# A last combine by column halves, and a gate unit whose products run as three passes

## The reference

```python
def expert_choice_ffn(h, w_router, w_gate, w_up, w_down):
    aff = softmax(h @ w_router)                          # 512 x 16
    gates, idx = top_k(aff.T, 64)                        # 64 tokens for each expert
    xe = h[idx]
    ye = (silu(xe @ w_gate[e]) * (xe @ w_up[e])) @ w_down[e]
    return zeros_like(h).at[idx].add(ye * gates)

x = x + expert_choice_ffn(rms_norm(x, norm_ffn), w_router, w_gate, w_up, w_down)
g = sigmoid(rms_norm(x, norm_ple) @ w_ple_gate)          # 1024 x 1024: the "gate unit"
e = rms_norm(p @ w_ple_proj, norm_ple_post)
x = x + g * e
```

## Time and profile before

| what | us |
|---|---|
| median of 3 executions | 2024.95 |
| lowest and highest of them | 2019.79, 2026.97 |
| span of the profiled execution, first to last instruction | 2020.3 |
| PE busy | 1916.6 |
| DVE busy | 842.5 |
| ACT busy | 577.4 |

### The profile page before, as it was taken

How to read it: one execution, slowest core, us unless ns; L and a number is a source line. 1 busy time by engine, 2 the same in 40 slices (tenths; PEclk the granted TensorE clock), 3 DMA queues, 4 the chain that set the end, 5 groups by cost and what they waited for, 6 DMA issues and landing times.

```text
span 2020.3 us, 22646 instructions
## 1 busy us (share of the span) xinstructions
PE 1916.6 (95%) x9101; PEld 1138.6 (56%) x9101; DVE 842.5 (42%) x1264; ACT 577.4 (29%) x912; POOL 37.4 (2%) x40
## 2 busy tenths in 40 slices
PE   8999899999999989899998999999999999999999
PEld 6667533332233233223323377888888788778887
DVE  6885511111111101111111166466566675886544
ACT  5563400000000000000000055443133434357761
POOL 1022000000000000000000000000000000000000
PEclk9999899999999999999999999999999999999999
DMA  8533699999999999999999954545245222221101
GB/s 268 167 100 138 250 403 429 428 429 428 429 429 428 429 428 430 428 429 429 428 429 428 422 177 159 184 153 190 87 166 172 80 85 82 84 74 53 43 22 42
DMA packets 105109, 528.13 MB, mean 261 GB/s; under 512 B 6998, under 2 KB 52884, under 8 KB 80340
## 3 DMA queue, kind: packets, MB, share of 16 engines
q1 hardware_dynamic: 102420, 520.55, 64.4%
q0 software_dynamic: 1008, 3.52, 0.7%
q10 hardware_dynamic: 1616, 3.15, 0.4%
HBM read 524.97 MB, written 2.23 MB: 261 GB/s over the span
## 4 chain that ended last, share of the span: by engine, by line
PE 68%; DMA 21%; DVE 6%; ACT 3%; issue 1%; ACTq 0%; DVEq 0%
DMA w_expert<-in_w_up 21%; PE bank L1206 11%; PE bank L1195 8%; PE bank L941 5%; PE bank L943 5%; PE bank L942 5%; PE bank L918 5%; PE bank L920 5%; PE bank L919 5%; PE bank L1168 3%; DVE full L1954 2%; PE bank L960 1%; DVE w_lo L1874 1%; PE bank L1418 1%; PE bank L1216 1%
## 5 line engine op out<-in xcount | busy, mean ns | idle before, releaser
L1195 PE MATMUL bank<-w_expert,chosen 128*64 128x512 f32 x2048 | 468.3, 598 | 59.5 <-DMA w_expert<-in_w_up 44.0
L1195 PEld LDWEIGHTS bank<-w_expert,chosen 128*64 128x64 f32 x2048 | 136.8, 136 | 372.0 <-issue 271.3
L2154 DVE TENSOR_TENSOR x_res<-x_res,bank 128x512 f32<-128x512 f32 x136 | 87.1, 683 | 422.4 <-PE bank L1216 402.3
L1206 PE MATMUL bank<-w_expert,hidden_t 128*64 128x512 f32 x1024 | 226.8, 595 | 4.6 <-ACT hidden_t L1662 4.6
L1874 DVE TENSOR_TENSOR w_lo<-raw,w_hi 128x2048 fp32r<-128x2048 f32 x74 | 170.2, 2301 | 113.0 <-ACT w_hi L1465 113.0
L1465 ACT CAST w_hi<-raw 128x2048 fp32r<-128x2048 f32 x74 | 141.0, 1905 | 129.3 <-PE bank L943 123.4
L2176 DVE TENSOR_TENSOR hidden_rows<-gate_silu,bank 128x512 f32<-128x512 f32 x32 | 20.5, 684 | 350.4 <-PE bank L1195 350.4
L918 PE MATMUL bank<-act_hi,w_hi 128*128 128x512 f32 x408 | 166.2, 407 | 0.1
L920 PE MATMUL bank<-act_hi,w_lo 128*128 128x512 f32 x408 | 159.1, 390 | 0.0
L919 PE MATMUL bank<-act_lo,w_hi 128*128 128x512 f32 x408 | 159.0, 390 | 0.0
L1206 PEld LDWEIGHTS bank<-w_expert,hidden_t 128*64 128x64 f32 x1024 | 75.6, 137 | 132.5 <-issue 123.6
(11 more groups left out here) (321 smaller groups left out, 2494.1 us busy)
## 6 DMA issues: line engine op xcount, KB each, us to landing
w_expert<-in_w_gate SPq DMA_DIRECT2D x64, 2048.0 KB, 35.3
w_expert<-in_w_up SPq DMA_DIRECT2D x64, 2048.0 KB, 32.4
w_expert<-in_w_down SPq DMA_DIRECT2D x64, 2048.0 KB, 34.1
raw<-in_a_w_in SPq DMA_DIRECT2D x24, 1024.0 KB, 6.6
raw<-in_b_w_in SPq DMA_DIRECT2D x16, 1024.0 KB, 5.3
raw<-in_a_ada_w SPq DMA_DIRECT2D x12, 1024.0 KB, 5.3
raw<-in_b_ada_w SPq DMA_DIRECT2D x12, 1024.0 KB, 6.0
raw<-in_kv_ada_w SPq DMA_DIRECT2D x8, 1024.0 KB, 5.4
```

The lines of the kernel that those rows point to most:

```text
L1195: last = mm(PS[b0 + n][HALF[x], :], XE[:, k % 4, HALF[k // 4]], WE[place][:, c0:c0 + 512], start=(k == 0), stop=(k == KD - 1), skip_group_ ...
L1206: last = mm(PS[4][HALF[x], :], HT[:, 4 * q + k, HALF[half]], WE[place][:, c0:c0 + 512], start=(i == 0 and k == 0), stop=(i == 7 and k == 3 ...
L2154: tt(part, part, ps[:, :], ALU.add).then_inc(d_add, 1)
```

## The change

Four things are changed. (1) The last expert's combine runs its eight matmuls by half first and then by tile, so that bank j holds half j // 4 and tile j % 4. (2) DVE's eight adds follow that order (`by_half=True`); inside the loop nothing changes. (3) norm(2) waits for as many adds as its column half needs: four before chunks 0 to 3 and eight before chunks 4 to 7, whatever the tile. (4) The first gate unit is no longer `tm_unit` but `first_gates`: for each slab three passes, high by high, high by low, low by high. Within a pass the chunks kc are outside and the four tiles inside. The first pass waits for `hi_ready` and `f_hi`, the second for `lo_ready`, the third for `f_lo`. `begin` is called for each tile at the very first chunk. Banks, slabs, semaphores and the count of 96 matmuls are as before.

```diff
@@ norm(k)
                         if k == 2:
-                            pe.wait_ge(d_add, ADDS - 8 + max(chunks[-1] + 1, 2 * t + 2))
+                            pe.wait_ge(d_add, ADDS - 8 + chunks[-1] + 1)
@@ behind the expert loop, PE
-            for t in range(NT):
-                for x in range(2):
-                    mm(PS[2 * t + x][:, :], SELT[HALF[x], t * P:(t + 1) * P], Y[HALF[x], :], start=True, stop=True
+            for x in range(2):
+                for t in range(NT):
+                    mm(PS[NT * x + t][:, :], SELT[HALF[x], t * P:(t + 1) * P], Y[HALF[x], :], start=True, stop=True
                        ).then_inc(m_c, 1)
             norm(2)
-            for h in range(2):
-                tm_unit(W_PGATE[h], [("pgate", h, t) for t in range(NT)], AH, AL, from_lo(18) if h == 0 else None)
+            def first_gates():
+
+                banks = []
+                for s in range(2):
+                    w = W_PGATE[0][s]
+                    hi, lo = w_hi(w), w_lo(w)
+                    pe.wait_ge(hi_ready, w + 1)
+                    for n, (x, weights) in enumerate(((AH, hi), (AH, lo), (AL, hi))):
+                        if n == 1:
+                            pe.wait_ge(lo_ready, w + 1)
+                        for kc in range(4 * s, 4 * s + 4):
+                            if n != 1:
+                                pe.wait_ge(f_lo if n else f_hi, 18 + kc + 1)
+                            for t in range(NT):
+                                key = ("pgate", 0, t)
+                                if s == 0 and n == 0 and kc == 0:
+                                    banks.append(begin(key, ends_next=False))
+                                last = mm(banks[t][:, :], x[:, kc, t * P:(t + 1) * P], weights[:, kc % 4 * 512:(kc % 4 + 1) * 512],
+                                          start=(s == 0 and n == 0 and kc == 0), stop=(n == 2 and kc == KD - 1))
+                                if n == 2 and kc == KD - 1:
+                                    ends(key)
+                                    last.then_inc(filled, 1)
+                    if s == 0:
+                        last.then_inc(half_used, 1)
+
+            first_gates()
+            tm_unit(W_PGATE[1], [("pgate", 1, t) for t in range(NT)], AH, AL)
@@ DVE
-            def add_combined(j, base_, ps):
+            def add_combined(j, base_, ps, by_half=False):
 
-                t, h = j // 2, j % 2
+                t, h = (j % NT, j // NT) if by_half else (j // 2, j % 2)
                 dve.wait_ge(m_c, base_ + (j + 1))
@@ DVE, behind the expert loop
             for j in range(8):
-                add_combined(j, 8 * NE, PS[j])
+                add_combined(j, 8 * NE, PS[j], by_half=True)
             split_upto(W_PGATE[0][0])
```

## The result

The changed kernel has a median of 2026.57 us over 14 executions (2022.5 to 2029.43), the kernel before 2022.9 over 14 (2019.79 to 2026.97). The ratio is 1.0015 with a 95% interval of 1.0008 to 1.0022: 3.0 us slower, between 1.6 and 4.5 (the two medians lie 3.7 apart). That is within 0.3%, as forecast, and on the slow side.

What follows compares the result with a forecast made beforehand. The prediction took PE, waiting at the seam for DVE's queue, to bound the kernel. Combine 0.96 plus banks 1.33 gave +2.3 us on a median of 2024.95, so 2027.2, range 2021.1 to 2031.9.

Steps and rivals of the forecast that it cites:

- The bound: At the seam PE waits for DVE's gapless queue of adds, slab and remainders, which sets when the first gate unit starts.
- Part 1: Last combine: the new order breaks PE's side-by-side pairs, so DVE's last add starts 0.96 us later.
- the two overlap cases: Last combine: last add 0.79 us later with full overlap of the halves, 0.96 if PE starts matmuls in order.
- the middle case: Last combine: matmuls start in order, only the halves' neighbours overlap; combine 6.0 us, last add 0.96 later.
- the signs given: Timeline marks expected afterwards, among them a combine of about 6.2 us with drain and eight adds of about 5.8.
- rival (b): Seam: first pass starts on ACT's chunks and the combine is not stretched; 1.1 us faster, 2023.8; chance 0.04.
- Part 2: Adds and norm(2): earlier waits gain nothing; transposes begin when PE's combine ends and take 3.6 us.
- Part 3: First gate pass: matmuls 1 to 4 each wait for a remainder to free their bank, 0.669 us apart; 1.33 lost.
- rival (c): Gate unit: granted clock falls to its lower level between 1169 and 1197; 2029.0, or 2049 if lasting; chance 0.06.
- Part 4: Behind the first unit: sigmoids come in a burst, but the second unit's second slab keeps 2.8 us of slack.
- The sum: Whole kernel: 0.96 for the combine plus 1.33 for the banks, +2.3 us, giving 2027.2; chance 0.70.
- the low stretch at norm(3): Low clock behind PE's idle time at 1216.7 to 1221.06: its length left open, worth up to 1.75 us either way.

Runs made afterwards that it cites:

- e6: Kernel before with passes, tiles outside in the very first, low weights last, remainders of chunks 0 to 3 before the first slab's low part; ratio 0.9993, seam 51.90 us.
- e4: Changed kernel with PE issuing the last combine in pairs of both halves as before, DVE still adding the first half first; one execution, 2027.03 us.
- e2: Kernel before with only the first gate unit replaced by the three passes, old combine kept; ratio 1.0011, seam 53.88 us.
- e5: Changed kernel with the last combine issued two matmuls of one half, then two of the other, in turn; one execution, 2023.58 us.
- e3: Changed kernel with the four tiles outside and the chunks inside in the very first pass; ratio 1.0010, seam 53.45 us.
- e1: Changed kernel with the old first gate unit, keeping the new combine, adds and norm(2) waits; ratio 1.0003, seam 53.46 us.
- e7: The changed kernel itself, run once more against the kernel before; ratio 1.0014, seam 54.66 us.
- e8: Kernel before with nine more matmuls at the start of the first gate unit, a mere shift; ratio 1.0021, seam 54.69 us.

## Why the prediction was right, and where it wasn't

**The bound.** Right: the chain through DVE's queue is what sets the start of the gate unit, before and after. e6 shows it from the other side: with the remainders moved up, the unit starts 0.8 sooner.

**Part 1, the combine: 0.96 forecast, 0.77 to 0.79 measured.** The size lies at the lower of the two overlap cases that I had worked out ("with full overlap of the two halves 0.79 later"), and the step that picked the middle case failed: PE doesn't start these matmuls strictly in order. The price of a lone matmul of 64 partitions, 0.86, was read rightly off rows 6 and 7: the adds come 0.86 apart while the first half runs alone. (The drain in rows 6 is 0.27, as between 3.70 and 3.43, and not 0.16.) Of the signs given, the combine takes 5.50 and not 6.2, and DVE's eight adds, with their gaps, 5.66 and not 5.8. What I had wrong is the cause behind the number. I put the cost down to pairs that the new order breaks on PE. e4 keeps the pairs and pays the same. The working had this in it (0.79 even with full overlap) and I didn't draw the conclusion: the order of the adds costs, and the order of the matmuls next to nothing. For the same reason rival (b) was wrongly put: it would have failed with the pairs intact.

**Part 2, adds and norm(2) by halves.** Right: the transposes begin as the combine ends and take 3.7, and nothing is gained. They begin 5.43 behind the combine's start, where 6.1 was forecast, as the combine is shorter.

**Part 3, the passes: 1.33 forecast, 1.27 measured** (44.87 from the unit's start to the spatial weights, 43.60 before; 1.26 in e2). The list of banks told it before any run. The number is closer than the step: matmuls 1 to 4 start 0.57, 0.66 and 0.66 apart, and not 0.67 each. That is 1.13 more than before, not 1.33, and the thirteen behind them add 0.14 that the forecast didn't have. The clock did not fall within the unit (rival (c)): the passes come 3.63 apart, 0.227 a matmul, and the granted clock reads 1.00 in each window from 1170.8 to 1194. On the rule of the Trainium skill that I had weighed (TensorE: Matmul & The Clock Gate, section A second HAM failure mode) this kernel is thus no case of it, with three holes of 0.34 to 0.43 and a change of bank at every matmul.

**Part 4, behind the unit.** Right: the low part of the second unit's second slab is done at 1201.94, and PE needs it 10.9 behind 1193.97, at 1204.9. The slack is 2.9 where 2.8 was forecast. The timelines of ACT and then of DVE in the changed kernel:

```profile
1193.49 1.27 ACT L1714 ACTIVATE square<-bank,stats 128x512 f32<-128x512 f32 x2 [8.23 <-PE bank L1288]
1195.80 0.69 ACT L1714 ACTIVATE square<-bank,stats 128x512 f32<-128x512 f32 x1 [1.04 <-DVE x_res L2228]
1197.12 0.69 ACT L1714 ACTIVATE square<-bank,stats 128x512 f32<-128x512 f32 x1 [0.64 <-DVE x_res L2228]
1197.71 1.91 ACT L1491 CAST w_hi<-raw 128x2048 fp32r<-128x2048 f32 x1
```
```profile
1199.65 2.29 DVE L1900 TENSOR_TENSOR w_lo<-raw,w_hi 128x2048 fp32r<-128x2048 f32 x1
```

**The sum and the time.** From the first combine matmul to the unit's last one I forecast 32.9, and it is 32.66 (the last pass starts at 1190.34, its last matmul 3.40 later); as a difference to the start of the second unit, +2.3 was forecast and +2.03 came. The time of 2027.2 against 2026.57 is closer than the reasoning deserves, and by luck. The three executions that I started from had a median of 2024.95; over 14 it is 2022.9, so that 2.05 of the agreement is the start point. From 2022.9 the same step would have given 2025.2. I also took the profiled execution to lie 4.65 under the median. Every later run gives its time beside its span, and the time is 1.75 to 1.87 more. That execution took about 2022.1, then, and lay 2.8 under.

The sum went to the seam only and left what comes behind it out, but for the low stretch at norm(3), which was kept for the range "worth up to 1.75 either way". The profiles show 2.04 at the seam and 0.3 to 0.5 behind it. That their total of 2.4 to 2.5 is so near to the 2.3 is thus luck too: two terms a little too large and one put at nothing.

## What to carry to other kernels

When a step is reordered so that a consumer takes all of one kind first, ask at what pace that kind is produced: two streams in turn may feed an engine that neither feeds alone, whatever the producer's total. When a unit is split so that its first part needs less, list every wait that its first instructions carry, the bank or buffer hand-over too; an input that is early is worth nothing while the output's place is still being read. And when one engine's queue is what all wait for, move what isn't urgent back in that queue, as e6 did with 2.28 us of low weights, before making the others wait for less. Measure such a step from its own start to a fixed point behind it, and then to the end: here executions differ by up to 5.8 us before they reach it.

## What the runs showed of the hardware

**A matmul of the other half may pass a waiting one.** In the changed kernel's combine PE's records (two for each matmul, 0.43 apart) stand alone at first and in twos from the third matmul of the first half on. Two short windows of the timeline, in the first matmul and in the third (columns as above):

```profile
1161.08 0.66 PE L1265 MATMUL bank<-expert_out,sel_gated_t 64*128 64x512 f32 x1 [0.73 <-issue]
```
```profile
1162.87 0.70 PE L1265 MATMUL bank<-expert_out,sel_gated_t 64*128 64x512 f32 x2
```

The third matmul of the first half starts at 1162.87, four records behind the first, and in the same window a second record runs. It isn't the fourth of the first half: its bank would be full with the third's, and DVE's fourth add would follow at DVE's own pace of 0.60, but it comes 0.86 behind the third and waits 0.17 for its bank. So the first matmul of the second half runs ahead of it. The whole is twelve steps of 0.43 and a drain, not fourteen, and e5's order, in which each pair has to pass one waiting matmul, is fully paired at 3.78. The Trainium skill (TensorE: Matmul & The Clock Gate, section Packing small matmuls) says that matmuls start strictly in order and only weight loads are pulled ahead. For float32 matmuls over 64 partitions, each of which is two records, the trace doesn't agree. It passed one waiting matmul here and not two (else the second half would have begun beside the second matmul of the first); no run tried more, or matmuls of one record.

**The low stretch of the clock behind an idle time goes with the kernel's schedule.** Before the transposes of norm(3) PE idles 4.32 or 4.33 in every one of these profiles, and yet the 32 transposes behind it take between 5.07 and 6.43. The ten profiles fall into groups by their seam, though they reach this stage at times that lie up to 5.9 us apart:

| seam | kernels | 32 transposes of norm(3) | 20 transposes before the dilated layer |
|---|---|---|---|
| 51.90, 52.62 | e6, before | 5.38, 5.38 | 2.40, 2.40 |
| 53.45, 53.46 | e3, e1 | 5.09, 5.07 | 4.04, 4.07 |
| 53.88 | e2 | 6.43 | 3.98 |
| 54.64 to 54.67 | changed, e7, e4, e5 | 6.10, 6.11, 6.06, 5.99 | 4.53, 4.53, 4.53, 3.53 |
| 54.69 | e8 | 5.89 | 3.43 |

The changed kernel gave the same lengths twice, with 2.1 us between the starts. So such a difference between two kernels can be real, and still be no price of the step that was changed. The length doesn't rise with the seam, and no run here shows by what rule it follows; the waits behind such a stretch take most of it back.
